# Two-layer hybrid encoder on one Trainium2 core: delta rule statistics and first matrices inside the short convolution's projection, later pieces in other slots

## The chip, the cores and the metric

The kernel runs on one core of a Trainium2 chip. The metric is the device time of one execution in microseconds (us). Engines are named as in the profile: PE (TensorE, matrix products; PEld its weight loads), DVE (VectorE), ACT (ScalarE), POOL (GpSimd) and SP (SyncE, which issues the loads of the weight stream).

## The reference, cut to what matters

The network has two layers, each a mixer, a cross attention over 256 memory rows and a squared-ReLU MLP, on 256 tokens of width 2048, all in float32. The change touches the even layer's mixer alone:

```python
def even_mixer(h, w_in, w_out, conv_qkv, a_log, dt_bias, out_gain, conv_sc):
    p = h @ w_in
    qkv = jax.nn.silu(centred_dwconv(p[..., :c1], conv_qkv))
    q = l2_normalize(q) * (DN_HEAD_DIM ** -0.5)
    k = l2_normalize(k)
    beta = jax.nn.sigmoid(ab[:, :, 0:2])
    g = -jnp.exp(a_log) * jax.nn.softplus(ab[:, :, 2:4] + dt_bias)
    o_fwd = gated_delta_rule(q, k, v, g[:, :, 0], beta[:, :, 0])
    o_bwd = flip(gated_delta_rule(flip(q), flip(k), flip(v), flip(g[:, :, 1]), flip(beta[:, :, 1])))
    ...
    y_sc = b_gate * centred_dwconv(c_gate * u_in, conv_sc)
    return jnp.concatenate([y_dn, y_sc], axis=-1) @ w_out
```

`gated_delta_rule` needs, for each chunk of tokens and each of 8 heads and 2 directions, the cumulative sums of g, the matrix `exp(diff)` of their differences, the products k k' and q k' scaled by it, and the inverse of the unit triangular matrix 1 + beta k k' exp(diff). With the inverse it runs over the chunks and carries a 128x128 state. The short convolution (`y_sc`) takes three other column blocks of the same projection and shares nothing with the delta rule but the output projection.

## The kernel before

**The weight stream.** All large products take their weights from one stream of units (128x1024 floats). SP loads them into a ring `raw`; for each unit ACT writes a rounded copy `split_hi` (`write_hi`, L330) when the unit four before it has been used, DVE writes the rest `split_lo` (`write_lo`, L337), and PE forms three reduced-precision products. PE counts used units in `s_used`. ACT and DVE run their other work between these copies, in the order in which the program lists it: `hi_upto(n)` and `lo_upto(n)` write the copies up to unit n, and what is listed behind them waits.

**The projection.** `pe_even` runs six chunks for q, k, v (`ev_qkv`), two for the gate, and six for the short convolution (`ev_sc`, `column_chunk`, L428 to L430). A chunk has 8 units of 24 matmuls of 128x256 each. Chunks use banks 0 and 1, or 2 and 3 of PSUM by turns; banks 4 to 7 (`aux`) are idle meanwhile. ACT takes chunks 0 and 3 of `ev_sc` (`cgate`), DVE multiplies chunks 1 and 4 into it (L1600) and convolves (L1535, L1539), and multiplies chunks 2 and 5 with the result (L1608).

**The head of the delta rule** stands behind the last chunk. PE turns k and v (L1284, 32 transposes), forms the cumulative sums (L1293) and the squared norms of q (L1299). ACT and DVE take the turned k and v (L1475, L1614), DVE squares k and sums it (L1619, L1620), and a chain of small operations on `st` ends in `s_stats`. Then come the first matrices of group 0: `pe_delta_pre` (L1370) broadcasts the cumulative sums and the betas by a product whose left side is one column of `decay_g` or `brk`, repeated 128 times, in float32 (pieces `cum` and `beta`), and forms k k' and k q' (pieces `kk` and `kq`). DVE makes the differences (`dve_delta_diff`, L1694), ACT their exponentials (`act_delta_pre`, L1516), DVE the products with beta (L1702), with q k' (L1704) and with k k' (`dve_delta_AT`, L1710). ACT copies the diagonal blocks (`act_delta_diag`), POOL masks them (L1097), DVE starts the inverse (`dve_inv_first`, L1173 and L1175).

**The four groups.** A group is two heads in both directions. `pe_inv` inverts its four matrices in six levels. In a level, for each direction, PE forms a product (L1108, 64x64 quadrants), ACT copies it (L1156), PE forms the second (L1135) and DVE subtracts it (L1193) and transposes (L1197); the last level is L1113, L1122, L1185. PE has four slots in a level (0 to 23 in a group), ACT and DVE two (0 to 11). Three tables say in which slots the other work goes: the tail of the group before (`pe_delta_tail`: five steps, L1388, L1394, L1400, L1406, L1417 to L1419), and the pieces of the next group.

```python
DN_PE = {'tail': (0, 2, 5, 7, 9), 'cum': (0, 12), 'beta': (6, 18), 'kk': (0,), 'kq': (10,)}
DN_ACT = {'tail': (0, 1, 3), 'pre': (4, 9), 'diag': (9, 11)}
DN_DVE = {'R': 1, 'out': 4, 'squares': 5, 'diff': (1, 7), 'masks': (5, 8), 'AT': (7, 9), 'first': (9, 11)}
```

The first number of a pair is direction 0's slot, the second direction 1's. POOL clears the inverse's two areas (L1202), masks, multiplies q (L1760) and makes the values of a group (L1748).

## Time and profile before

| what | value |
|---|---|
| time, median of 3 runs | 2865.39 us (2865.32 to 2878.22) |
| time of the profiled execution | 2865.1 us |
| its span | 2863.3 us |
| PE busy | 2766.4 us (97%), 18050 matmuls |
| PEld busy | 2430.6 us (85%) |
| DVE busy | 1555.8 us (54%) |
| ACT busy | 1303.0 us (46%) |
| POOL busy | 119.6 us (4%) |
| chain that ended last | PE 91%, DVE 5%, ACT 2%, issue 1% |

The share of the busy time of PE says little here, since its matmuls overlap and since the whole kernel is a string of stages. What an edit is worth stands in the chain of waits of its own stage: for the even mixer that is from 216.8 us, where the short convolution's projection starts, to 527.2 us, where the output projection does.

### The profile page before, as it was taken

How to read it: one execution, taken by the hardware profiler on the slowest of the kernel's cores; microseconds unless marked ns; L12 is line 12 of the kernel's file. 1: busy time of each engine (PE TensorE's matmuls, PEld its weight loads, DVE VectorE, ACT ScalarE, POOL GpSimd, SP SyncE). 2: the span in 40 equal slices, each digit the busy share in tenths (PEclk: the TensorE clock that was granted, in tenths of full speed). 3: DMA queues.
4: the chain of work that ended last, by engine and by line, in shares of the span. 5: the costliest groups of instructions: out<-in, count | busy, mean ns of one | idle time of the engine just before them, and what ended most of it. 6: DMA issues, size and time to landing. Idle time of an engine off the chain costs nothing.

```text
span 2863.3 us, 44423 instructions
## 1 busy us (share of the span) xinstructions
PE 2766.4 (97%) x18050; PEld 2430.6 (85%) x18050; DVE 1555.8 (54%) x2080; ACT 1303.0 (46%) x1726; POOL 119.6 (4%) x167
## 2 busy tenths in 40 slices
PE   8999989999999999999999998799999999999999
PEld 8999978778888888888899898688888888888887
DVE  5555455575555555555544556654654555555554
ACT  4543333464553544435444444333654445354453
POOL 0000033000000000000000000250000000000000
PEclk9999987899999999999999999897999999999999
DMA  7455400444455555555544554002534555555554
GB/s 277 164 189 189 165 2 2 156 173 143 170 191 195 188 196 179 202 193 180 195 141 173 194 191 159 1 2 75 183 144 173 190 180 200 197 187 193 185 187 146
DMA packets 67801, 461.71 MB, mean 161 GB/s; under 512 B 7023, under 2 KB 10223, under 8 KB 13084
## 3 DMA queue, kind: packets, MB, share of 16 engines
q1 hardware_dynamic: 63824, 449.46, 43.8%
q10 hardware_dynamic: 3500, 5.21, 0.5%
q0 software_dynamic: 288, 4.19, 0.4%
q8 instruction: 158, 2.59, 0.4%
q14 instruction: 31, 0.25, 0.0%
HBM read 456.72 MB, written 5.27 MB: 161 GB/s over the span
## 4 chain that ended last, share of the span: by engine, by line
PE 91%; DVE 5%; ACT 2%; issue 1%; DMA 0%; ACTq 0%; POOL 0%; DVEq 0%; POOLq 0%
PE bank L405 17%; PE bank L386 13%; PE bank L388 13%; PE bank L387 13%; PE bank L407 9%; PE bank L428 5%; PE bank L430 5%; PE bank L429 5%; PE bank L1108 1%; PE bank L1135 1%; PE bank L1370 1%; DVE split_lo L337 1%; PE bank L2227 1%; ACT split_hi L330 0%; DVE hT L578 0%
## 5 line engine op out<-in xcount | busy, mean ns | idle before, releaser
L337 DVE TENSOR_TENSOR split_lo<-raw,split_hi 128x1024 fp32r<-128x1024 f32 x840 | 1019.7, 1224 | 964.2 <-ACT split_hi L330 963.9
L330 ACT ACTIVATE split_hi<-raw 128x1024 fp32r<-128x1024 f32 x840 | 881.1, 1058 | 1168.6 <-PE bank L388 576.3
L405 PE MATMUL bank<-hT,split_hi 128*128 128x512 f32 x2048 | 716.1, 394 | 1.5 <-DVE hT L578 1.5
L407 PE MATMUL bank<-hT,split_lo 128*128 128x256 f32 x2048 | 573.7, 280 | 0.7 <-issue 0.7
L405 PEld LDWEIGHTS bank<-hT,split_hi 128*128 128x128 f32 x2048 | 383.8, 187 | 92.1 <-issue 2.3
L386 PE MATMUL bank<-split_hi,u_hi 128*128 128x512 f32 x1152 | 449.4, 390 | 0.0
L388 PE MATMUL bank<-split_hi,u_lo 128*128 128x512 f32 x1152 | 448.4, 389 | 0.0
L387 PE MATMUL bank<-split_lo,u_hi 128*128 128x512 f32 x1152 | 448.3, 389 | 0.0
L407 PEld LDWEIGHTS bank<-hT,split_lo 128*128 128x128 f32 x2048 | 386.6, 189 | 1.8 <-issue 1.7
L428 PE MATMUL bank<-hT,split_hi 128*128 128x256 f32 x1328 | 377.8, 284 | 3.1 <-DVE hT L578 1.8
L430 PE MATMUL bank<-hT,split_lo 128*128 128x256 f32 x1328 | 377.2, 284 | 0.0
L429 PE MATMUL bank<-hT,split_hi 128*128 128x256 f32 x1328 | 377.1, 284 | 0.0
L428 PEld LDWEIGHTS bank<-hT,split_hi 128*128 128x128 f32 x1328 | 256.4, 193 | 3.7 <-DVE hT L578 2.0
L429 PEld LDWEIGHTS bank<-hT,split_hi 128*128 128x128 f32 x1328 | 256.3, 193 | 0.2
L430 PEld LDWEIGHTS bank<-hT,split_lo 128*128 128x128 f32 x1328 | 256.3, 193 | 0.0
L388 PEld LDWEIGHTS bank<-split_hi,u_lo 128*128 128x128 f32 x1152 | 216.2, 188 | 45.1
L387 PEld LDWEIGHTS bank<-split_lo,u_hi 128*128 128x128 f32 x1152 | 216.3, 188 | 44.6
L386 PEld LDWEIGHTS bank<-split_hi,u_hi 128*128 128x128 f32 x1152 | 216.3, 188 | 44.5
L386 PE MATMUL bank<-split_hi,hT 128*128 128x512 f32 x448 | 175.9, 393 | 1.9 <-DVE split_lo L337 1.3
L387 PE MATMUL bank<-split_lo,hT 128*128 128x512 f32 x448 | 175.0, 391 | 0.0
L388 PE MATMUL bank<-split_hi,hT 128*128 128x512 f32 x448 | 174.8, 390 | 0.0
L386 PEld LDWEIGHTS bank<-split_hi,hT 128*128 128x128 f32 x448 | 84.5, 189 | 20.4 <-DVE split_lo L337 2.2
(446 smaller groups left out, 2336.3 us busy)
## 6 DMA issues: line engine op xcount, KB each, us to landing
raw<-in_stream SPq DMA_DIRECT2D x420, 1024.0 KB, 4.8
work<-in_mem POOLq DMA_DIRECT2D x2, 2048.0 KB, 8.4
bias_rows<-bias_line SPq DMA_DIRECT2D x1, 3072.0 KB, 14.2
hwork<-bias_rows ACTq DMA_DIRECT2D x2, 1536.0 KB, 9.8
x<-in_x SPq DMA_DIRECT2D x1, 2048.0 KB, 9.2
out<-x SPq DMA_DIRECT2D x4, 512.0 KB, 5.0
rwork<-in_wide ACTq DMA_DIRECT2D x1, 1280.0 KB, 13.9
const<-in_masks SPq DMA_DIRECT2D x1, 1121.5 KB, 13.5
```

What stands on the lines that cost most here:

```text
L330: nc.scalar.activation(split_hi[:, u % SPLIT], raw[:, b % RAW, (u % 2) * UNIT:(u % 2 + 1) * UNIT], ACT.Copy).then_inc(s_hi, 1)
L337: nc.vector.tensor_tensor(split_lo[:, u % SPLIT], raw[:, b % RAW, (u % 2) * UNIT:(u % 2 + 1) * UNIT], f32(split_hi[:, u % SPLIT]), SUB).th ...
L386: nc.tensor.matmul(out, lhsT=x_hi, rhs=w_hi[:, cols], start=k == 0, stop=False)
L387: nc.tensor.matmul(out, lhsT=x_hi, rhs=w_lo[:, cols], start=False, stop=False)
L388: m = nc.tensor.matmul(out, lhsT=x_lo, rhs=w_hi[:, cols], start=False, stop=k == k_tiles - 1)
L405: nc.tensor.matmul(out[:, :], lhsT=w_hi[:, cols], rhs=hT[:, k].rearrange("p two s -> p (two s)"), start=k == 0, stop=False)
L407: m = nc.tensor.matmul(out[:, S:2 * S], lhsT=w_lo[:, cols], rhs=hT_hi[:, k, :], start=False, stop=k == KD - 1)
L428: nc.tensor.matmul(out, lhsT=w_hi[:, cols], rhs=hT_hi[:, k, :], start=k == 0, stop=False)
L429: nc.tensor.matmul(out, lhsT=w_hi[:, cols], rhs=hT_lo[:, k, :], start=False, stop=False)
L430: m = nc.tensor.matmul(out, lhsT=w_lo[:, cols], rhs=hT_hi[:, k, :], start=False, stop=k == KD - 1)
L1108: i = nc.tensor.matmul(aux[d][rows, m * HALF:(m + 1) * HALF], lhsT=mask[rows, d, m, :], rhs=T[rows, d, m, :], start=True, stop=True)
L1135: i = nc.tensor.matmul(out, lhsT=lhsT, rhs=rhs, start=True, stop=True)
```

## The change

Five parts.

1. The transposes of v and of k, the cumulative sums, the squares of q and the statistics are done inside the six chunks of `ev_sc`. PE does a piece behind a given unit of a chunk (`pe_delta_head`); ACT and DVE have their share placed between copies of the stream (`hi_sc`, `lo_sc`). v is now taken by ACT (before: DVE). The banks are 4 to 7.
2. The broadcasts of the cumulative sums and the betas take another form, for all groups. Once for all heads and both directions, a float32 product writes the sums (and later the betas) as rows; ACT rounds them (`act_rows_hi`), DVE writes the rest to other partitions of the same tile `rowsT` (`dve_rows_lo`). A piece is then 2 reduced-precision products of 128x256, whose left side is a column of the constant `pick`, where it was 4 float32 products of 128x128.
3. Group 0's pieces are formed behind unit 3 of chunk 4 (`cum`, `beta`) and behind unit 0 of chunk 5 (`kk`, `kq`, in banks 0 and 1, once chunk 4 has been taken). Its differences, exponentials, masks and the start of its inverse go between the copies of chunks 4 and 5. POOL's first masks come ahead of its clearing, which waits for the end of the projection.
4. Buffers move, since the head's tiles may no longer lie over the stream's ring or over `hT`: they take the room of the memory's keys and values, which is free then (`mwork`).
5. In the slots of groups 1 to 3, direction 0's differences (DVE) go from 1 to 0, its beta (PE) from 6 to 2, the tail's third product (PE, L1400) from 5 to 3, and direction 0's diagonal (ACT) from 9 to 8.

```diff
-        DN_PE = {'tail': (0, 2, 5, 7, 9), 'cum': (0, 12), 'beta': (6, 18), 'kk': (0,), 'kq': (10,)}
-        DN_ACT = {'tail': (0, 1, 3), 'pre': (4, 9), 'diag': (9, 11)}
-        DN_DVE = {'R': 1, 'out': 4, 'squares': 5, 'diff': (1, 7), 'masks': (5, 8), 'AT': (7, 9), 'first': (9, 11)}
+        DN_PE = {'tail': (0, 2, 3, 7, 9), 'cum': (0, 12), 'beta': (2, 18), 'kk': (0,), 'kq': (10,)}
+        DN_ACT = {'tail': (0, 1, 3), 'pre': (4, 9), 'diag': (8, 11)}
+        DN_DVE = {'R': 1, 'out': 4, 'squares': 5, 'diff': (0, 7), 'masks': (5, 8), 'AT': (7, 9), 'first': (9, 11)}
...
+        def pe_delta_head(pe, c, u):
+            if (c, u) == (0, 1):
+                pe.wait_ge(s_silu, 6)
+                pe.wait_ge(s_abv, 2)
+                pe_delta_turn(pe, dn_vT)
+            elif (c, u) == (1, 2):
+                pe_delta_turn(pe, dn_kT, taken=True)
+            elif (c, u) == (2, 2):
...
+                m.then_inc(s_head_pe, 1)
+            elif (c, u) == (4, 0):
+                pe.wait_ge(s_stats, 1)
+                pe.wait_ge(s_kv_a, 8)
+                for t in range(NT):
+                    m = nc.tensor.matmul(aux[3][:, t * P:(t + 1) * P], lhsT=eightfold(brk_rows, t), rhs=ident, start=True, stop=True)
+                m.then_inc(s_head_pe, 1)
+            elif (c, u) == (4, 3):
+                pe.wait_ge(s_head_act, 1)
+                for d in range(2):
+                    for piece in ("cum", "beta"):
+                        pe_delta_pre(pe, 0, d, piece)
+            elif (c, u) == (5, 0):
+                wait_chunks_taken(pe, starts["ev_sc"][0] + 5)
+                for piece in ("kk", "kq"):
+                    pe_delta_pre(pe, 0, 0, piece)
...
+            if hp == 1 and piece == "kk":
+                wait_chunks_taken(pe, after("ev_sc"))
...
+                if piece in ("cum", "beta"):
+                    own = pick[:, 8 * d + h:8 * d + h + 1].broadcast_to([P, P])
+                    m = nc.tensor.matmul(out[:, i * S:(i + 1) * S], lhsT=own, rhs=rowsT[:, d if piece == "cum" else 2, :],
+                                         start=True, stop=True)
+                    continue
...
+            lo_sc(4, 5)
             for d in range(2):
                 dve_delta_diff(dve, 0, d)
-                dve_delta_masks(dve, 0, d)
+            lo_sc(4, 8)
+            for d in range(2):
+                dve_delta_DB(dve, 0, d)
+            take_gated(4)
+            for d in range(2):
+                lo_sc(5, 1 + d)
+                dve_delta_QKT(dve, 0, d)
+            for d in range(2):
+                lo_sc(5, 3 + d)
                 dve_delta_AT(dve, 0, d)
             for d in range(2):
                 dve_inv_first(dve, 0, dn_inv[0], d)
+            take_output(5)
...
         def pool_even(pool):
-            pool.wait_ge(s_stats, 1)
+            pool_delta_masks(pool, 0)
+            wait_chunks_taken(pool, after("ev_sc"))
             for Tf in dn_Tt:
                 m = pool_clear(Tf)
             m.then_inc(iv_clear, 1)
-            pool_delta_masks(pool, 0)
```

Three places show how the rows move. The first is PE behind the last matmul of the projection, before: all of the head, then group 0's first product (L1108). A float32 product counts once in these rows and is two instructions in the trace; a transpose counts once in both.

```order
L1284 MATMUL bank<-const,work 128x128 x32
L1293 MATMUL bank<-st,const 128x8 x8
L1299 MATMUL bank<-const,hwork 128x1 x16
L1370 MATMUL bank<-const,st 128x128 x8
L1370 MATMUL bank<-work 128x128 x8
L1370 MATMUL bank<-const,st 128x128 x8
L1108 MATMUL bank<-work 64x64 x8
L1370 MATMUL bank<-const,st 128x128 x4
L1370 MATMUL bank<-work 128x128 x4
L1108 MATMUL bank<-work 64x64 x8
```

The same place now (L436 to L438 are the projection's matmuls, L1116 the inverse's first product, L1423 the new broadcasts, L1428 k k'):

```order
L437 MATMUL bank<-hT,split_hi 128x256
L438 MATMUL bank<-hT,split_lo 128x256
L1116 MATMUL bank<-work 64x64 x8
L1423 MATMUL bank<-rowsT,pick 128x256 x2
L1428 MATMUL bank<-work 128x128 x4
L1116 MATMUL bank<-work 64x64 x8
L1143 MATMUL bank<-work 64x32 x8
L1423 MATMUL bank<-rowsT,pick 128x256 x2
L1143 MATMUL bank<-work 64x32 x8
```

Nothing of the head is left between the projection and the inverse; it stands between units of the projection, as this one, behind unit 2 of chunk 2 (sums, rows, squares of q):

```order
L438 MATMUL bank<-hT,split_lo 128x256
L1366 MATMUL bank<-st,const 128x8 x8
L1372 MATMUL bank<-const,work 128x128 x4
L1378 MATMUL bank<-const,mwork 128x1 x16
L436 MATMUL bank<-hT,split_hi 128x256
```

The second place is DVE in chunk 5, now (L345 copies of the stream, L1805 and L1811 group 0's products with q k' and k k', L1181 and L1183 the start of its inverse, L1688 the taking of chunk 5):

```order
L345 TENSOR_TENSOR split_lo<-raw,split_hi 128x1024
L1805 SCALAR_TENSOR_TENSOR mwork<-bank,st,mwork 128x128 x4
L345 TENSOR_TENSOR split_lo<-raw,split_hi 128x1024
L1811 SCALAR_TENSOR_TENSOR mwork<-bank,st,mwork 128x128 x4
L345 TENSOR_TENSOR split_lo<-raw,split_hi 128x1024
L1811 SCALAR_TENSOR_TENSOR mwork<-bank,st,mwork 128x128 x4
L1181 TENSOR_TENSOR work<-const,work 128x256
L1183 STREAM_TRANSPOSE work<-work 128x256
L1181 TENSOR_TENSOR work<-const,work 128x256
L1183 STREAM_TRANSPOSE work<-work 128x256
L1688 TENSOR_TENSOR work<-work,bank 128x512 x2
```

Both starts of the inverse stand ahead of the taking of chunk 5, where before they stood behind it and behind the whole head.

The third place is PE in the first two levels of group 1, before:

```order
L1388 MATMUL bank<-hwork,rwork 128x128 x4
L1370 MATMUL bank<-const,st 128x128 x4
L1370 MATMUL bank<-work 128x128 x4
L1108 MATMUL bank<-hwork,work 64x64 x8
L1135 MATMUL bank<-work,hwork 64x32 x8
L1394 MATMUL bank<-hwork 128x128 x4
L1135 MATMUL bank<-work,hwork 64x32 x8
L1108 MATMUL bank<-hwork,work 64x64 x16
L1400 MATMUL bank<-hwork,work 128x128 x4
L1135 MATMUL bank<-work,hwork 64x32 x8
L1370 MATMUL bank<-const,st 128x128 x4
L1135 MATMUL bank<-work,hwork 64x32 x8
```

and now (L1447, L1453, L1459 are the tail's first three steps):

```order
L1447 MATMUL bank<-hwork,rwork 128x128 x4
L1423 MATMUL bank<-rowsT,pick 128x256 x2
L1428 MATMUL bank<-work 128x128 x4
L1116 MATMUL bank<-hwork,work 64x64 x8
L1143 MATMUL bank<-work,hwork 64x32 x8
L1453 MATMUL bank<-hwork 128x128 x4
L1423 MATMUL bank<-rowsT,pick 128x256 x2
L1143 MATMUL bank<-work,hwork 64x32 x8
L1459 MATMUL bank<-hwork,work 128x128 x4
L1116 MATMUL bank<-hwork,work 64x64 x16
```

The third step of the tail comes ahead of the second level's first products, and each broadcast is 2 rows of 128x256 where it was 4 of 128x128.

## Rows read from the trace of the kernel before

**Rows 1.** Busy time in stretches; columns: us, PE, PEld, DVE, ACT, POOL, PEclk, DMA share, GB/s

```profile
216.80:355.00 138.20, 138.20 (x1153) 138.11 (x1151) 69.45 (x76) 50.62 (x51) 0.00 (x0) 1.00 0.51 180
355.00:383.10 28.10, 16.28 (x129) 15.93 (x129) 18.18 (x44) 11.66 (x18) 3.24 (x4) 0.81 0.00 1
383.10:407.40 24.30, 22.02 (x434) 20.26 (x434) 16.89 (x52) 8.60 (x22) 13.27 (x20) 0.92 0.01 3
407.40:443.70 36.30, 34.29 (x490) 31.82 (x490) 20.60 (x60) 11.43 (x29) 13.31 (x20) 0.78 0.01 2
```

**Rows 2.** The chain of waits between projection and inverse: start us, us, what

```profile
355.15 1.30 DVE work L1608 x2
...
356.69 3.70 PE bank L1284 x32
...
369.17 5.45 PE bank L1370 x32
```

**Rows 3.** Timeline of PE in the head: start us, us, engine, line, shapes, count

```profile
360.22 1.85 PE L1293 MATMUL bank<-st,const 128*128 128x8 f32 x16
361.92 3.71 PE L1299 MATMUL bank<-const,hwork 128*128 128x1 f32 x32
...
372.66 1.95 PE L1370 MATMUL bank<-work 128*128 128x128 f32 x16
```

**Rows 4.** The chain of waits in the projection: one matmul of 128x256

```profile
340.00 0.12 PE bank L428
```

**Rows 5.** Timeline of DVE about the end of chunk 4

```profile
334.35 1.28 DVE L1600 TENSOR_TENSOR work<-work,bank 128x512 f32<-128x512 f32 x2
335.66 1.14 DVE L1535 TENSOR_SCALAR work<-work,par 128x256 f32<-128x256 f32 x4
336.84 3.38 DVE L1539 SCALAR_TENSOR_TENSOR work<-work,par 128x256 f32<-128x256 f32 x8
```

**Rows 6.** Timeline of DVE in the head: product of group 0 with beta

```profile
379.32 0.69 DVE L1702 TENSOR_TENSOR rwork<-rwork,bank 128x512 f32<-128x512 f32 x1 [0.77 <-ACT rwork L1516]
```

**Rows 7.** Timeline of ACT: a change of function and what follows it

```profile
77.00 1.28 ACT L1436 ACT_TABLE_LOAD   x1
78.29 1.06 ACT L1436 ACTIVATE work<-work 128x1024 f32<-128x1024 f32 x1
```

**Rows 8.** Timeline of POOL, head and group 0

```profile
369.26 0.95 POOL L1202 MEMSET rwork<- 128x1024 f32 x1 [368.42 <-DVE st L1632]
...
384.53 1.58 POOL L1760 TENSOR_TENSOR hwork<-work,hwork 128x256 f32<-128x256 f32 x2
386.07 2.77 POOL L1097 TENSOR_TENSOR work<-iv_diag,const 128x256 f32<-128x256 f32 x4
```

**Rows 9.** The chain of waits in groups 0 to 3

```profile
388.92 1.07 PE bank L1108 x32
...
410.51 3.28 PE bank L1370 x16
...
419.25 1.09 PE bank L1370 x8
...
436.02 2.02 PE bank L1370 x8
```

**Rows 10.** Busy time in stretches of one granted clock; columns as in rows 1

```profile
386.80:406.80 20.00, 18.32 (x404) 16.66 (x402) 15.01 (x49) 7.63 (x20) 9.63 (x15) 1.00 0.01 2
...
413.70:434.00 20.30, 18.90 (x343) 17.31 (x344) 11.77 (x34) 5.02 (x12) 6.66 (x11) 1.00 0.01 2
434.00:447.70 13.70, 13.10 (x144) 12.31 (x139) 8.82 (x27) 6.25 (x16) 4.53 (x7) 0.50 0.01 2
447.70:468.40 20.70, 19.30 (x328) 17.71 (x329) 10.95 (x31) 4.67 (x11) 8.78 (x14) 0.99 0.01 3
468.40:488.70 20.30, 19.69 (x244) 18.33 (x244) 11.12 (x34) 7.72 (x19) 9.75 (x14) 0.50 0.00 1
488.70:505.80 17.10, 14.05 (x300) 12.80 (x297) 10.91 (x24) 7.09 (x13) 4.01 (x7) 1.00 0.04 7
```

More of the change, by code:

```diff
@@ L214, in R, with M @@
             return view(rwork, at, *shape)
+        def M(at, *shape):
+            return view(mwork, at, *shape)
         def four(ap):
@@ L1591, in dve_even, with lo_sc, take_gated @@
             dve.wait_ge(s_silu, 6)
-            for half in range(2):
-                c = 3 * half + 1
+            def lo_sc(c, used):
+                lo_upto(dve, min(chunk_done("ev_sc", c - 1) + used + AHEAD, starts["ev_out"][1]))
+            def take_gated(c):
                 banks, taken = chunk_banks("ev_sc", c)
-                lo_upto(dve, chunk_done("ev_sc", c - 1) + AHEAD)
-                lo_upto(dve, chunk_done("ev_sc", c) + AHEAD)
                 wait_chunks_taken(dve, starts["ev_sc"][0] + c)
```

218 lines of the change are left out of this document (129 added, 89 removed).

## The prediction, made before the changed kernel was run

> **What bounds the kernel now.** I read the busy time in stretches first, to see which part of the even mixer leaves PE without work. The projection of the short convolution has none to give: PE is busy for all of its 138.20 us at a granted clock of 1.00, while DVE is busy for 69.45 us, ACT for 50.62 and POOL not at all [rows 1]. The 28.1 us behind it are the opposite: PE 16.28, DVE 18.18, each waiting for the other, and no DMA [rows 1]. The chain of waits through this stretch is the second view: it goes from DVE's taking of the last chunk over PE's transposes (3.70 us) to the float32 broadcasts and products (5.45 us), with DVE and ACT between [rows 2]. Nothing in it needs the projection's result, but it stands behind it. Third, the chain through the groups: from the second level on it runs mostly over PE, and the broadcasts stand in it with 1.09 to 3.28 us each [rows 9]. So PE sets the end in the projection and mostly in the groups, and the head is a string of waits that could lie beside the projection.
>
> **The head goes away: 28.1 us off.** A sixth of the projection is 23.03 us, a unit 2.88 us. ACT and DVE need about half of that for the copies. If group 0's inverse is started when chunk 5 ends, PE goes from the last unit straight to its first product. Counted from the end of chunk 5's unit 4, DVE has one copy, one product with k k', ACT two diagonals, POOL the masks and DVE two starts to do; none is longer than 3 us, and 4 units (11.5 us) cover them. If that cover were gone the start would come late by what is missing, up to some 6 us.
>
> **What PE does instead, inside the projection: 13.4 us on.** PE has no idle time there, so each of its instructions counts in full. The 32 transposes take 3.70 [rows 2]. The sums (x16) took 1.85 and the squares (x32) 3.71; by their starts 1.70 and 3.7 [rows 3]. Products of 128x128 in float32 cost 1.95 us for 16 instructions at full clock, 0.12 each [rows 3]: the rows of the sums are 8 instructions, 0.96; the rows of the betas 4, 0.48; `kk` and `kq` 16, 1.95. The new broadcasts are 8 products of 128x256 in the projection's own form, at 0.12 each [rows 4]: 0.96. Together 13.45 us. No row shows this form with a single repeated column on its left side; at the least it costs nothing, at the most what the float32 form costs, 3.9 us for the 32 instructions it replaces. I take the projection's row, since type and shape are the same.
>
> **A new wait at the third piece: 2.2 us on.** `kk` and `kq` of group 0 write banks 0 and 1, so PE waits behind unit 0 of chunk 5 until DVE has taken chunk 4. Chunk 4 ends at 216.8 + 5 x 23.03 = 331.95. The taking ran from 334.35 to 335.63 [rows 5]; now two products with beta of 0.69 us stand ahead of it [rows 6], so it ends at 337.0. PE is there at 331.95 + 2.88 = 334.8. That is 2.2 us of idle PE; the whole rest of the projection is queued behind it. Bounds: 0, if ACT's and DVE's copies keep their times and the products with beta get ahead of the last copy; and 5, if ACT's exponentials push its copies back by their own length.
> ACT changes function three more times in the projection's time. A change took 1.28 us, and the next activation began 1.29 us after its start [rows 7]. The Trainium skill, ScalarE: Activation LUTs, section What ACT_TABLE_LOAD costs, puts a switch at about 2.66 us, with a drain behind the load. The trace does not agree for this kernel: the row has no drain in it. By the page the copies ahead of the taking would come about 1 us later and the sum would be 1 us less of a gain.
>
> **Do the copies of the stream stay ahead?** A copy may start once the unit four before it is used, and PE needs it three units, 8.6 us, later. The longest new stretch without a copy on DVE is two products with beta, the taking (1.28) and the convolution (1.14 and 3.38) [rows 5, 6], 7.2 us, begun 2.4 us behind chunk 4's end; it ends at 9.6, the next copy is done by 10.9, and PE needs it at 11.5 without the wait above and at 15.7 with the wait and the 1.95 of `kk` and `kq`. I cost it at nothing; the cover is 0.6 to 4.8 us.
>
> **Group 0: 2.0 us off.** Its first product starts at full clock, but POOL's clearing must now wait for the end of the projection. From there: taking of chunk 5 1.3 and a hand-over of 0.15 [rows 2], two clearings of 0.95, two products of q 1.58, the first mask of level 2 at 2.77 / 4 = 0.7 [rows 8]: 5.6 us. Before, level 2 began at 388.92, 5.8 us behind the first product at 383.1 [rows 1, 9], so the start gives nothing; POOL is late next. Two broadcasts leave the path of levels 2 to 4, 8 instructions and 1.09 each before, now nothing (it falls into POOL's wait) and 0.24: 1.9 us. The last third of the group is DVE's, and DVE's work is the same.
>
> **Groups 1 and 2: 3.2 us off each.** In slot 0 broadcast and `kk` took 3.28 us, half of it for each at mostly half clock [rows 9]; `kk` stays, the broadcast becomes 0.5: 1.0 off. Direction 0's beta was 1.09, now 0.4: 0.7 off. Direction 1's beta was 2.02, with DVE waiting for it, now 0.5: 1.5 off [rows 9]. Direction 1's sums lie beside DVE's work and count as nothing. Group 2 repeats the pattern. Of the moved slots, the differences and the third product feed waits on DVE and ACT that are not on the chain while PE is; I cost them at nothing, between a gain of 1 us per group and the same as a loss. Group 3 has no pieces of a next group: nothing.
>
> **The clock: 3.3 us on.** The granted clock in the groups changes between its two levels, 2.4 GHz (1.00) and 1.2 GHz (0.50). In group 1 it was 0.50 for 13.7 us and in group 2 to 3, where fewer and smaller products stand, for 20.3 us, with PE busy for 13.10 and 19.69 of them [rows 10]. It fell each time behind a stretch at 1.00 in which PE had been idle for 1.4 us in all (18.90 of 20.30, 19.30 of 20.70) [rows 10], and rose late. The change takes 128x128 work out of just these stretches. I charge the difference of these two stretches once, 6.6 us at half clock, 3.3 us. The bounds are a gain of 6.6 (the first of them vanishes, half of 13.10) and the last rival below.
>
> **Sum:** -28.1 + 13.45 + 2.2 - 2.0 - 2 x 3.2 + 3.3 = -17.5 us. The profiled execution took 2865.1 us, so 2847.6; the median of the runs, 2865.39, is the same within 0.3 us. A measurement of this kernel can tell about 0.5%, 14.3 us, from no change.
>
> **The rivals.**
> B, the groups give nothing: DVE's chain closes up behind what PE gives back. For it: DVE is busy for 16.89 of 24.30 us in group 0 and 20.60 of 36.30 in group 1 [rows 1], and the end of each group is its own. Against it: the chain's own rows are PE's. 2865.1 - 28.1 + 13.45 + 2.2 = 2852.7.
> C, the clock helps: denser groups keep the full clock through the first of the slow stretches, and nothing is charged. 2847.6 - 3.3 - 6.6 = 2837.7. For it, only that the idle time in the stretches that ended in a fall was short, 1.4 us, and may close.
> D, the stream starves: with a cover of as little as 0.6 us, some of the five stretches of head work on DVE and ACT overrun it by about 1 us each, and the clock falls once more. 2847.6 + 5 + 3.3 = 2855.9. Against it, DVE is half idle there [rows 1].
> E, slower: the clock stays at half level through the groups. Its place is the four stretches of 20.0, 20.3, 20.7 and 17.1 us at 1.00, in which PE was busy for 70.6 us [rows 10]. Less the 8.4 us taken out, 62 us of PE's work would take twice as long: 2847.6 + 62 = 2910. It outweighs the gain once some 18 of these 62 us are lost. For it: the 0.50 from group 2's end on lasted 20.3 us, with PE busy for 19.69 of them [rows 10]. Against it: the clock rose in group 3 too, at 488.7, where no piece of a next group stands [rows 10]. The Trainium skill, TensorE: Matmul & The Clock Gate, section What's actually happening, says that the throttled state is the default and that activity releases it. By that rule, less work on PE speaks for E; the trace agrees so far as the longest stretch at 0.50 is the one with the fewest products of 128x128.
>
> **How the numbers follow.** Forecast A 0.62, B 0.14, C 0.12, D 0.07, E 0.05. The likeliest is A, 2847.6, with its own range from 2841 (no wait at the third piece, no charge for the clock) to 2852 (the wait at 5 us, the moved slots a small loss). The range for 8 in 10 reaches beyond it, to 2836 for C and to 2856 for D: left out are E, half of D and half of C, 0.15. Faster by over 0.5% (below 2851) are A but for 0.06, C and a little of B: 0.70. Within 0.5% are the rest of A, B and D: 0.26. Slower is E but for 0.01: 0.04.
>
> **What would show it.** In the profile of the changed kernel the stretch between the last 128x256 matmul of the projection and the first 64x64 product should be below 0.5 us; the projection should last 138.2 + 13.45 + 2.2 = 153.9 us, with one idle time of PE of about 2 us at the k k' product that DVE's taking of chunk 4 ends; PE should wait in level 2 of group 0 for POOL's mask, by about 1 us; the new broadcasts should read 0.12 us each at clock 1.00; and groups 1 and 2 should last about 33 us each instead of 36.3. Waits of the projection's matmuls for `split_lo` would show D, a clock of 0.50 where rows 10 have 1.00 would show E. The forecast is wrong if the time is outside 2836 to 2856.

## The result, and the profile of the changed kernel

The changed kernel took 2855.08 us (median of 9 runs, 2852.31 to 2861.01), the kernel before in the same comparison 2866.44 us (9 runs). The ratio is 0.995, with a 95% interval of 0.9936 to 0.9964. A second comparison on another chip gave 2855.38 us against 2868.89 us, 0.9958 (0.9944 to 0.9972). So the change gains 11 to 14 us, 0.4 to 0.5%. The forecast was 17.5 us. The time lies inside the range of 2836 to 2856 us, at its slow end.

The page of the changed kernel: span, busy time, clock in 40 slices, and the chain by engine.

```profile
span 2851.4 us, 44270 instructions
PE 2762.2 (97%) x17966; PEld 2421.5 (85%) x17966; DVE 1555.6 (55%) x2080; ACT 1305.0 (46%) x1733; POOL 119.6 (4%) x167
PEclk9999996899999999999999999897999999999999
PE 92%; DVE 4%; ACT 2%; issue 1%; DMA 0%; ACTq 0%; POOL 0%; DVEq 0%; POOLq 0%
```

The profiled execution took 2853.17 us, 11.9 us less than that of before. PE's busy time fell by 4.2 us only, since most of what went was waiting and the head's work moved rather than went. The seventh clock slice reads 6: the groups' clock has its own part in what follows.

The busy time in stretches, the changed kernel: the projection with the head in it, then groups 0 to 3. They answer to [rows 1]; columns as there.

```profile
215.80:372.70 156.90, 154.73 (x1271) 154.36 (x1272) 86.33 (x119) 64.19 (x75) 3.07 (x4) 0.98 0.45 159
372.70:395.96 23.26, 19.00 (x408) 16.67 (x409) 16.65 (x52) 8.74 (x23) 13.53 (x20) 0.96 0.01 3
395.96:429.10 33.14, 29.63 (x464) 27.03 (x465) 20.49 (x60) 11.28 (x28) 13.32 (x20) 0.81 0.01 2
429.10:463.01 33.91, 31.24 (x464) 28.82 (x464) 20.67 (x60) 11.27 (x28) 13.32 (x20) 0.75 0.01 2
463.01:513.78 50.77, 44.29 (x497) 40.84 (x498) 20.10 (x44) 17.61 (x33) 12.34 (x18) 0.60 0.11 43
```

And the two last of them in the kernel before, which [rows 1] does not reach:

```profile
443.70:479.46 35.76, 33.76 (x489) 31.39 (x489) 20.60 (x60) 11.14 (x28) 13.30 (x20) 0.79 0.01 2
479.46:527.20 47.74, 40.06 (x497) 36.47 (x498) 19.85 (x44) 17.61 (x33) 12.35 (x18) 0.69 0.12 45
```

The ledger, from [rows 1] and these rows:

| stretch | before | after | difference | forecast |
|---|---|---|---|---|
| projection and head | 166.3 | 156.9 | -9.4 | -12.45 |
| group 0 | 24.3 | 23.3 | -1.0 | -2.0 |
| group 1 | 36.3 | 33.1 | -3.2 | -3.2 |
| group 2 | 35.8 | 33.9 | -1.9 | -3.2 |
| group 3 and last tail | 47.7 | 50.8 | +3.0 | 0 |
| the groups' clock | | | (in the rows above) | +3.3 |
| all else | | | +0.6 | 0 |
| span | 2863.3 | 2851.4 | -11.9 | -17.5 |

Two places lost what was not foreseen: the projection, which now runs at a granted clock of 0.98 instead of 1.00, and group 3, whose clock went from 0.69 to 0.60. The chain of waits of the changed kernel shows the first, and the foreseen waits beside it (start us, us, what):

```profile
274.21 1.69 PE bank L1366 x16
275.89 0.99 PE bank L1372 x8
276.88 5.31 PE bank L1378 x32
...
332.99 0.91 PE bank L1423 x8
...
349.13 1.30 DVE work L1678 x2
350.47 2.05 PE bank L1428 x16
...
372.71 1.29 DVE work L1688 x2
374.12 0.95 POOL rwork L1210
375.07 0.89 POOL work L1210
375.95 1.38 POOL hwork L1861 x2
377.33 0.69 POOL work L1105
378.16 0.68 PE bank L1116 x16
...
399.08 0.43 PE bank L1423 x2
399.51 1.70 PE bank L1428 x8
...
456.64 0.74 PE bank L1423 x2
```

L1366 are the sums, L1372 the rows and L1378 the squares of q. The squares took 5.31 us, where they took 3.71 [rows 3]. The broadcasts (L1423) are 8 products in 0.91 us. Behind the squares the matmuls of the projection take 0.21 us each up to 285.2 us, and 0.12 again from there. L1428 (`kk`, `kq`) stands behind DVE's taking of chunk 4 (L1678), and the first level-2 product (378.16) behind POOL's clearings, products and mask, as the forecast has it.

What PE waited for between 215 and 515 us, changed kernel: us in total, times, longest.

```profile
PE bank L1116 <- DVE hwork L1201: 3.2, 3, 2.0
...
PE bank L1428 <- DVE work L1678: 2.2, 1, 2.2
...
PE bank L1116 <- POOL work L1105: 0.8, 1, 0.8
```

No matmul of the projection waited for `split_lo` or `split_hi`: the stream did not starve. Here is the clock in one stretch in which PE does nothing but the later squares, in one behind it with the projection's own matmuls, and in one of the same length a little later:

```profile
278.60:282.19 3.59, 3.59 (x18) 3.59 (x18) 0.00 (x0) 0.00 (x0) 0.00 (x0) 0.50 0.54 224
282.20:285.50 3.30, 3.30 (x18) 3.30 (x19) 0.00 (x0) 0.00 (x0) 0.00 (x0) 0.57 0.00 0
286.00:289.30 3.30, 3.30 (x29) 3.30 (x29) 1.70 (x2) 1.06 (x1) 0.00 (x0) 1.00 0.00 0
```

PE reads as busy for all three. The clock is at its lower level in the first and in most of the second. The squares cost 1.6 us more than their row. Behind them 18 matmuls are counted in 3.3 us where 29 are at full clock, 11 x 0.12 = 1.3 us more. Together 2.9 us, which is the projection's shortfall of 3.0 within 0.1.

### The profile page after: what moved, and what is told of

The parts are those of the page before. It is cut to its first block, busy times and chain, and to the rows that moved or that the text cites. A ratio compares the mean times of both kernels' runs of the same rounds, so it can differ in the third digit from the quotient of the medians.

```text
span 2851.4 us, 44270 instructions
## 1 busy us (share of the span) xinstructions
PE 2762.2 (97%) x17966; PEld 2421.5 (85%) x17966; DVE 1555.6 (55%) x2080; ACT 1305.0 (46%) x1733; POOL 119.6 (4%) x167
## 4 chain that ended last, share of the span: by engine, by line
PE 92%; DVE 4%; ACT 2%; issue 1%; DMA 0%; ACTq 0%; POOL 0%; DVEq 0%; POOLq 0%
PE bank L413 17%; PE bank L394 13%; PE bank L395 13%; PE bank L396 13%; PE bank L415 8%; PE bank L436 5%; PE bank L438 5%; PE bank L437 5%; PE bank L1116 1%; PE bank L1143 1%; ACT split_hi L338 1%; PE bank L2328 1%; DVE split_lo L345 1%; DVE hT L586 0%; PE bank L1982 0%
## 5 line engine op out<-in xcount | busy, mean ns | idle before, releaser
L345 DVE TENSOR_TENSOR split_lo<-raw,split_hi 128x1024 fp32r<-128x1024 f32 x840 | 1020.1, 1224 | 967.8 <-ACT split_hi L338 967.1
L436 PE MATMUL bank<-hT,split_hi 128*128 128x256 f32 x1328 | 377.5, 284 | 3.1 <-DVE hT L586 1.8
L438 PE MATMUL bank<-hT,split_lo 128*128 128x256 f32 x1328 | 376.3, 283 | 0.0
L436 PEld LDWEIGHTS bank<-hT,split_hi 128*128 128x128 f32 x1328 | 255.5, 192 | 3.7 <-DVE hT L586 2.0
L438 PEld LDWEIGHTS bank<-hT,split_lo 128*128 128x128 f32 x1328 | 255.4, 192 | 0.0
```

What stands on the lines that cost most here:

```text
L345: nc.vector.tensor_tensor(split_lo[:, u % SPLIT], raw[:, b % RAW, (u % 2) * UNIT:(u % 2 + 1) * UNIT], f32(split_hi[:, u % SPLIT]), SUB).th ...
L436: nc.tensor.matmul(out, lhsT=w_hi[:, cols], rhs=hT_hi[:, k, :], start=k == 0, stop=False)
L438: m = nc.tensor.matmul(out, lhsT=w_lo[:, cols], rhs=hT_hi[:, k, :], start=False, stop=k == KD - 1)
```

## The experiments

All times are medians with the ratio to the kernel before on the same chip, which itself read 2866.4 to 2869.4 us. The stretches come from each run's own profiled execution. "Half clock" is worked out from 1 us stretches as the sum of 2 x (1 - granted clock); "later" is what follows the output projection's start, which no kernel here changes. Where a text below gives the stretches of single groups, they run from the first product of one tail (L1447 in the changed kernel) to that of the next, about 1 us behind the group's own start, and the last one to the output projection.

| kernel | time | ratio (95%) | head | groups | half clock in them | later | half clock, second mixer |
|---|---|---|---|---|---|---|---|
| before | | | 166.4 | 143.8 | 64.5 | 2336.4 | 71.6 |
| after | 2855.08 | 0.995 (0.9936, 0.9964) | 156.8 | 140.8 | 71.4 | 2337.9 | 78.5 |
| after_again | 2855.38 | 0.9958 (0.9944, 0.9972) | 156.7 | 141.9 | 68.3 | 2338.2 | 78.5 |
| squares_split | 2851.18 | 0.9927 (0.9907, 0.9946) | 155.2 | 140.6 | 71.4 | 2340.7 | 85.4 |
| third_later | 2853.89 | 0.9941 (0.992, 0.9962) | 154.3 | 140.1 | 71.6 | 2342.2 | 88.7 |
| both_head | 2850.95 | 0.995 (0.9932, 0.9968) | 151.2 | 140.1 | 71.5 | 2340.4 | 85.3 |
| old_slots | 2860.68 | 0.9971 (0.9952, 0.999) | 158.2 | 138.4 | 61.4 | 2345.0 | 99.0 |
| head_alone | 2862.36 | 0.9973 (0.9961, 0.9986) | 155.1 | 141.8 | 58.0 | 2342.8 | 78.5 |
| both_tail5 | 2852.04 | 0.9949 (0.9933, 0.9965) | 151.2 | 137.4 | 58.0 | 2346.5 | 99.0 |
| both_tail5_pool | 2853.43 | 0.9944 (0.9925, 0.9963) | 151.2 | 138.7 | 61.4 | 2343.7 | 99.0 |
| both_tail5_busy | 2847.52 | 0.9939 (0.9919, 0.9959) | 151.1 | 135.1 | 37.5 | 2340.1 | 71.7 |
| busy_wide | 2834.40 | 0.9883 (0.9862, 0.9904) | 151.2 | 128.2 | 13.6 | 2336.7 | 78.5 |
| before_busy | 2859.04 | 0.9967 (0.9949, 0.9985) | 166.4 | 132.7 | 20.3 | 2343.6 | 88.7 |
| after_busy | 2841.82 | 0.9908 (0.9886, 0.993) | 158.2 | 125.4 | 6.8 | 2336.0 | 75.1 |

The column "later" has to be read first. Nothing in it was changed, yet it varies by 10 us, and mostly with the half clock of the second layer's mixer. Between two kernels, the stretches of the head and the groups tell more than the medians do. In the table the groups end with the first matmul of the output projection, 0.3 us ahead of where the ledger's rows end. A ratio rests on 4 to 11 runs of a kernel; only the intervals of busy_wide and after_busy lie clear of that of the changed kernel.

**1. squares_split: the squares in four pieces, behind units 3 to 6.**

```diff
-                for t in range(NT):
-                    for h in range(DN_H):
+            elif c == 2 and u in (3, 4, 5, 6):
+                t = (u - 3) // 2
+                for h in range(4 * ((u - 3) % 2), 4 * ((u - 3) % 2) + 4):
```

> The 16 one-column products (squares of q) stand behind unit 2 of chunk 2 in one run; here four each stand behind units 3, 4, 5 and 6. In the trace of the changed kernel the granted clock is at 0.50 from 278.6 to 285.9 us, beginning 1.7 us into these products. Theory A (a run of products of one column lets the clock fall): the clock stays at 1.00 through the projection, the first 64x64 product of group 0 comes 3.4 us earlier after the projection's start (156.8 us to about 153.4), and the time falls by about 3 us. Rival B (the fall has another cause, the interruption of the stream as such or the moment): there is still a stretch at 0.50 of about 7 us in the projection, and the time is the same.

The head took 155.2 us, 1.6 less than the changed kernel and 1.8 more than expected. The clock stayed at 1.00 behind the squares, but fell for 3.4 us behind the wait for chunk 4 instead:

```profile
277.00:290.00 13.00, 13.00 (x114) 13.00 (x113) 9.31 (x7) 3.17 (x3) 0.00 (x0) 1.00 0.43 163
351.40:354.90 3.50, 3.50 (x19) 3.50 (x18) 3.43 (x10) 0.00 (x0) 0.00 (x0) 0.51 0.22 91
```

So the squares in one run are what lowers the clock at 278 us, and a second weak place lies behind it. The kept traces bear this out: the clock fell in or right behind the squares in all eight in which they stand in one run (the kernel before and before_busy among them), and in none of the six in which they stand in four pieces. At the wait of 2.2 us for chunk 4 it fell in three of six (squares_split, old_slots, after_busy). The squares follow directly on the sums, 16 instructions of 8 columns, and on the rows; whether the squares alone would lower the clock was not tried.

**2. third_later: `kk` and `kq` of group 0 one unit later.**

```diff
-            elif (c, u) == (5, 0):
+            elif (c, u) == (5, 1):
```

> Group 0's products k k' and k q' go from behind unit 0 to behind unit 1 of chunk 5. The wait of 2.2 us for DVE's taking of chunk 4 was 5.2 us behind the end of chunk 4, and unit 1 ends 5.8 us behind it. Theory A (the wait is only a matter of place): PE's wait goes, the projection with the head is 2.2 us shorter (156.8 to 154.6), nothing is later at the start of group 0, time 2 us less. Rival B (the wait moves on): DVE's products with q k' are pushed back behind the later PE products, the start of the inverse comes too late, and PE waits at the first 64x64 product instead; time the same or more.

The head took 154.3 us, 2.5 less, and the wait of 2.2 us is gone, as theory A has it; DVE's later work is still in time. The median fell by 1.2 us only. What remained before `kk` was a wait of 0.4 us for the taking of chunk 5, in group 1.

**3. both_head: both edits.**

> Both head edits together: the squares of q in four parts behind units 3 to 6 of chunk 2, and group 0's k k' and k q' behind unit 1 of chunk 5. Each alone left one stretch at half clock in the projection: with the squares in parts it came behind the 2.2 us wait (351 to 355), with the later third piece behind the squares (278 to 285). Theory A (both falls are set off by what stands just before them: a run of one-column products, a pause of PE of 2 us): no half clock between 216 and the inverse, projection with head 138.2 + 13.4 = 151.6 us (changed kernel 156.8), and about 5 us less in time than the changed kernel. Rival B (falls come at some rate whatever stands there): one stretch remains, 153.5 us or more.

The head took 151.2 us. This is its busy time in both_head:

```profile
215.90:367.10 151.20, 151.20 (x1271) 151.07 (x1271) 86.30 (x119) 64.42 (x75) 2.88 (x4) 1.00 0.46 164
```

And this one of the four pieces of the squares in the chain of waits of both_head:

```profile
279.77 0.79 PE bank L1380 x8
```

PE is busy throughout at a clock of 1.00, and 8 squares cost 0.79 us. The forecast's 138.2 + 13.45 without wait and clock is 151.65 us; the sum of the PE work is right within 0.5 us. Up to the output projection both_head is 6.3 us shorter than the changed kernel, and the later part was 2.5 us longer in the profiled run. The median is 4 us lower than on the changed kernel's chip, but the ratio to the kernel before is 0.995 in both: the gain is shown by the stretches and not by the times.

**4. old_slots: the four table moves undone, everything else of the change kept.**

```diff
-        DN_PE = {'tail': (0, 2, 3, 7, 9), 'cum': (0, 12), 'beta': (2, 18), 'kk': (0,), 'kq': (10,)}
+        DN_PE = {'tail': (0, 2, 5, 7, 9), 'cum': (0, 12), 'beta': (6, 18), 'kk': (0,), 'kq': (10,)}
```

(and `diag` from 8 to 9, `diff` from 0 to 1)

> The changed kernel with the tables of slots as before (third product of the tail in slot 5, beta in 6, direction 0's differences on DVE in 1, its diagonal on ACT in 9). I forecast nothing for the moved slots. Theory A: groups 0 to 2 the same within 0.5 us each, group 3 with its tail (50.8 us in the changed kernel, 47.7 before) the same, so that its 3.1 us of loss are the clock's. Rival B: the third product in slot 3 runs at the half clock in group 3 (2.0 us instead of 1.1) and causes the loss: group 3 comes back to 48 us here, and the time is 2 to 3 us less.

Groups 0 to 2 lasted 24.5, 33.1 and 34.1 us, those of the changed kernel 24.4, 33.1 and 33.9: the moves do nothing there. The last stretch lasted 46.7 us against 49.4: with the moves it is 2.7 us longer. Its head lasted 158.2 us, since the clock fell behind the squares and once more behind the wait for chunk 4. Even so old_slots is the quicker kernel by the stretches, by 1 us up to the output projection. By the medians it is the slower one (2860.68, the intervals overlap), and its granted clock over all its runs was 0.9696 on average against 0.9707. Whether the moves bring something through the later clock is not settled.

**5. head_alone: also the broadcasts of groups 1 to 3 in their old form.**

```diff
-                if piece in ("cum", "beta"):
+                if piece in ("cum", "beta") and hp == 0:
...
+                    if piece == "cum":
+                        lhsT = decay_g[:, t, 8 * d + h:8 * d + h + 1].broadcast_to([P, P])
+                        rhs = const_of("causal", 2 * d + 1)
```

> Groups 1 to 3 are as in the kernel before (float32 broadcasts of 4 products, the old slots); only the head and group 0's own matrices are inside the projection. Theory A (the sum by parts holds): groups 0 to 3 last what they lasted before, 24.3, 36.3, 35.8 and 47.7 us, so the kernel keeps the head's gain of 9.6 us alone, ratio to the kernel before 0.9966, and the clock in groups 1 to 3 has the stretches of before. Rival B (the groups' new form and slots give the net gain and the head little, or entering group 0 at full clock changes the pattern after it): the stages of the groups differ by more than 1 us each from before.

The stretches from group 0 on were 25.9, 35.6, 36.3 and 44.0 us, against 24.5, 33.1, 34.1 and 46.7 in old_slots. The new form takes 6.1 us off the groups in which it stands and gives 2.7 back in the last, which has none: net 3.4. The kernel before has 25.3, 36.3, 35.8 and 46.4 us by the same cuts, so the last stretch of head_alone is 2.4 us shorter than there with the same instructions in it, at 22.8 us of half clock against 28.6. Theory A fails there: what stands earlier shifts the clock of the groups. The head lasted 155.1 us, the clock behind the squares having fallen for only 3.4 us in this run instead of 6.8; that depth is not the program's alone.

**6. both_tail5: both_head, with the tail's third product back in slot 5.**

```diff
-        DN_PE = {'tail': (0, 2, 3, 7, 9), 'cum': (0, 12), 'beta': (2, 18), 'kk': (0,), 'kq': (10,)}
+        DN_PE = {'tail': (0, 2, 5, 7, 9), 'cum': (0, 12), 'beta': (2, 18), 'kk': (0,), 'kq': (10,)}
```

> As both_head, and of the four moved slots only the tail's third product back in slot 5. With all four undone the stretch from group 2's tail to the output projection was 46.7 us, against 49.4 in the changed kernel. Theory A (the third product in slot 3 is what costs group 3, where no piece of a next group stands): 46.7 us or less again, groups 0 to 2 as in the changed kernel, time 2.7 us below both_head. Rival B (it is one of the others, or the phase of the clock): 49 us again.

Group 3 with the last tail in both_head:

```profile
457.90:507.10 49.20, 42.87 (x482) 39.54 (x481) 20.04 (x44) 16.86 (x31) 12.21 (x18) 0.60 0.12 44
```

and in both_tail5:

```profile
457.70:504.40 46.70, 38.86 (x483) 35.38 (x481) 19.85 (x44) 16.87 (x31) 12.23 (x18) 0.69 0.12 46
```

This one move sets the clock of the last stretch: 0.69, as before the change, against 0.60. The stretch is 2.5 us shorter. The other traces agree: in the five with slot 3 and no unused products it has 39.0 to 39.5 us of half clock and lasts 49.2 to 50.4 us, in the five with slot 5 it has 22.8 to 29.1 us and lasts 44.0 to 46.8. The median did not follow (2852.04 against 2850.95), and the later part was 6.1 us longer in the profiled run.

**7. both_tail5_pool: also POOL's second clearing and its products with q behind the masks of levels 2 and 3 of group 0.**

```diff
-            for Tf in dn_Tt:
-                m = pool_clear(Tf)
+            pool_clear(dn_Tt[0])
...
+                    if hp == 0 and level == 3:
+                        pool_clear(dn_Tt[1]).then_inc(iv_clear, 1)
+                        for d in range(2):
+                            pool_delta_pre(pool, 0, d)
```

> As both_tail5, and POOL clears only the first area ahead of the masks of levels 2 and 3 of group 0; the second clearing and the two products of q come behind them. In the changed kernel PE waited 0.8 us for POOL's first mask of level 2, and the chain there went over POOL for 4 us. Theory A (POOL is what is late at the start of group 0): group 0 is 0.8 to 2 us shorter (23.3 to about 22). Rival B (DVE's differences in its slot 0 are as late as POOL): the wait goes over to DVE, group 0 the same.

The wait for POOL (0.8 us) is gone, and in its place stands one for DVE, kernel both_tail5_pool:

```profile
PE bank L1116 <- DVE work L1201: 0.6, 1, 0.6
```

The stretch from group 0's start to the first tail was 24.4 us instead of 24.8. POOL was late, but DVE was almost as late: 0.4 us at the most. Over the four groups nothing was won: 138.7 us against 137.4, with 3.4 us more of half clock in them.

**8. both_tail5_busy: both_tail5 with 16 unused float32 products of 128x256, four each in slot 19 of group 0 and slot 15 of groups 1 to 3.** Nothing is left out; `pe_keep_busy` issues products into a bank that nobody reads, and both kernels call it in other stages already.

```diff
+                    n = {(0, 19): 4, (1, 15): 4, (2, 15): 4, (3, 15): 4}.get((hp, slot), 0)
+                    pe_keep_busy(bank[1], n)
```

> As both_tail5, with four unused float32 products of 128x256 (1.7 us at full clock) in PE's pause of each group: slot 19 of group 0, slot 15 of groups 1 to 3. They write a free bank; nothing reads it. Theory A (PE's pause of 1.5 to 2 us lets the clock fall and the fall costs the groups several us each): the stretches at half clock behind the pauses (7, 14 and 21 us in groups 1, 2 and 3) go or shrink, groups 1 to 3 are 3 to 6 us shorter each, time 8 us or more below both_tail5. Rival B (the thin mix of 64x64 products lets it fall whether PE pauses or not): the same stretches at half clock, and the time is up by what the products delay, 0 to 3 us.

Half clock in the groups fell from 58.0 to 37.5 us and their time from 137.4 to 135.1, though PE has more to do. The expected 3 to 6 us for each of groups 1 to 3 did not come: the four stretches are 25.6, 32.1, 33.8 and 43.6 us against 24.8, 32.6, 33.3 and 46.7, so the last alone gains. The median fell by 4.5 us where 8 were expected; the two intervals overlap.

**9. busy_wide: both_tail5_pool with 21 such products at six slots and one behind each of the last tail's first four steps.**

```diff
+                    n = {(0, 19): 3, (1, 15): 4, (1, 19): 3, (2, 15): 4, (2, 19): 3, (3, 15): 4}.get((hp, slot), 0)
...
+                if step < 4:
+                    pe_keep_busy(bank[3], 1)
```

> As both_tail5_pool, with unused float32 products in both pauses of PE in every group (slot 19: three, in groups 0 to 2; slot 15: four, in groups 1 to 3) and one behind each of the last four waits of the last tail. With fillers in one pause of each group the half clock from the projection to the output projection went from 58.0 to 37.5 us and the stretch from 288.6 to 286.2 us. Theory A (pauses of 1.6 us let the clock fall in each group): less than 20 us at half clock, stretch 280 us or less, granted clock of the whole run 0.980 or more, and by the slope of 19 us of time for 0.01 of clock that the runs of every kernel here show, a time of about 2843. Rival B (the remaining falls come from the thin mix of 64x64 products): still 35 us or more at half clock, and the stretch is longer by what the fillers delay.

**10. after_again: the changed kernel on the same chip, as a yardstick.**

> The changed kernel itself once more, so that it stands beside busy_wide on one chip. Theory A: stages as in the first trace within 0.5 us each up to the output projection (projection with head 156.8, groups 33.1 and 33.9, last stretch 49.4), the half clock in the projection behind the squares again; the time differs by what the second layer's mixer, untouched by the change, spends at half clock. Rival B: the stages themselves move by several us from run to run.

busy_wide took 2834.40 us, 0.9883 (0.9862 to 0.9904), and beats both kernels: 21 us less than after_again (2855.38), 34 less than before. It is 9 us faster than expected; half clock in the groups is 13.6 us and the stretch from the projection to the output projection 279.4 us, as theory A has it. In after_again the head and groups 0 to 2 lasted what they had lasted in the first trace within 0.2 us, but the last stretch 50.4 us instead of 49.4, and the half clock in groups 1 to 3 lies in other places. So a stretch of one trace can move by 1 us with nothing changed. All this left open whether the products need the change.

**11 and 12. before_busy and after_busy: the 25 products of experiment 9 (the texts of the expectations count the 21 in the slots as 18) in the kernel before, and in the changed kernel, with no other edit.**

> The kernel before with the wide set of unused products in the groups (18 at six slots, 4 in the last tail), nothing of the change in it. Theory 1, the products act only through the clock of the groups and the gain has nothing to do with the change: the 75 us at half clock between 200 and 520 us fall to below 35 us, of which most stand in group 1 to 3; the stretches of the groups get shorter by some 14 us together and the time is 2866 - 14 = 2852 us. Theory 2, the products help only where the new broadcasts have taken the float32 ones away (four float32 products of 128x128 keep the clock by themselves, so that there is less to win): the half clock stays above 55 us and the time is 2860 us or more.

> The changed kernel with the same wide set of unused products in the groups and no other edit. Theory 1: the head keeps its two losses (squares at half clock, wait for chunk 4, together 5.6 us), the third product its slot 3, the groups and the last tail run as with the full set: 2834.4 + 5.6 + up to 2.5 = 2840 to 2843 us. Theory 2, slot 3 and the POOL order matter more than the clock: above 2848 us.

Groups 0 to 3, kernel before_busy:

```profile
383.20:408.00 24.80, 23.88 (x454) 21.78 (x454) 16.89 (x52) 8.97 (x23) 13.29 (x20) 0.94 0.01 3
408.00:439.90 31.90, 31.09 (x509) 27.90 (x503) 20.42 (x60) 11.30 (x28) 13.34 (x20) 1.00 0.01 2
439.90:471.70 31.80, 30.99 (x504) 27.88 (x502) 20.41 (x60) 11.24 (x28) 13.33 (x20) 1.00 0.01 3
471.70:515.90 44.20, 38.40 (x500) 33.92 (x497) 19.42 (x44) 16.67 (x33) 12.36 (x18) 0.81 0.12 49
```

and kernel after_busy:

```profile
375.00:398.80 23.80, 20.83 (x431) 18.17 (x430) 16.65 (x52) 9.15 (x24) 13.54 (x20) 1.00 0.01 3
398.80:429.50 30.70, 28.64 (x483) 25.36 (x479) 20.39 (x60) 11.33 (x28) 13.34 (x20) 1.00 0.01 2
429.50:460.10 30.60, 28.54 (x480) 25.34 (x478) 20.39 (x60) 11.23 (x28) 13.33 (x20) 1.00 0.01 3
460.10:500.40 40.30, 34.51 (x500) 30.32 (x496) 19.49 (x44) 16.44 (x32) 12.35 (x18) 0.92 0.15 54
```

By the half clock theory 1 holds: it fell to 20.3 us in the kernel before, and the products act through the clock, with or without the change. They take 11.1 us off the groups of before and 15.4 off those of after. The median of before_busy, 2859.04 us, is 7 us above what was expected, and close to theory 2's 2860; 2.9 us of that are missing in the groups (11.1 instead of 14), and the later part was 7.2 us longer in the profiled run (2343.6 against 2336.4 us). after_busy, 2841.82 us, is where theory 1 put it.

The rows also show what the change does to a group when the clock stays up: groups 1 and 2 last 30.7 and 30.6 us instead of 31.9 and 31.8, 1.2 us less each. With the products in both kernels the change is worth 15.5 us up to the output projection, as against 12.6 without them: part of its gain had gone into the clock. The medians give 17.2 us (2859.04 to 2841.82) as against 11 to 14, but on 8 and 4 runs and with later parts that differ by 7.6 us. Slot 3 for the third product is no loss here. Group 3 with the last tail lasts 40.3 us with slot 3, and 41.8 in busy_wide with slot 5, where it has 3.4 us more of half clock. A kernel with both_head's two edits and after_busy's groups was not tried.

## Why the prediction was right in part

**The head: right.** The stretch between the projection and the inverse is gone: its last matmul starts at 372.4 us, the first 64x64 product at 372.6 (forecast below 0.5 us apart). The 28.1 us went.

**The work on PE inside the projection: right in amount, wrong in one term.** Sums 1.69 us (forecast 1.70), rows 0.99 (0.96), broadcasts 0.91 (0.96); both_head's 151.2 us for the whole. The failed term is "the squares (x32) 3.71". The row was taken over as a duration, as if the place did not matter. The squares took 5.31 us and the matmuls behind them 1.3 us more than at full clock, since the clock fell during the squares; together 2.9 us. Here lies the miss in the head. The trace of before held the warning. These are a stretch inside the squares there, which ended at 365.63 us, one right behind them, and the longer one up to `kk` and `kq` at 372.66 us:

```profile
363.60:365.60 2.00, 2.00 (x19) 1.95 (x18) 1.97 (x2) 1.02 (x1) 0.00 (x0) 1.00 0.00 0
365.70:367.70 2.00, 0.00 (x0) 0.00 (x0) 1.97 (x3) 0.00 (x0) 0.00 (x0) 0.51 0.00 0
365.00:373.00 8.00, 4.46 (x26) 4.38 (x26) 4.80 (x13) 2.00 (x3) 1.84 (x2) 0.57 0.00 0
```

The clock had fallen there too, within 0.1 us of their end and ahead of the 3.5 us in which PE then stood idle, so the pause is not what set it off. What that cost lay inside the 28.1 us that were to go, and I read only the duration.

**The wait at the third piece: right.** 2.2 us forecast, 2.2 measured, from the same releaser; third_later took it away.

**The copies stay ahead: right.** No wait for the stream. The change of ACT's function at 293.34 us again took 1.28 us with the next activation 1.30 us behind its start, as in [rows 7]. This is its row and the next, the timeline of ACT in the changed kernel:

```profile
293.34 1.28 ACT L1546 ACT_TABLE_LOAD   x1
294.64 0.26 ACT L1546 ACTIVATE st<-st 128x64 f32<-128x64 f32 x1
```

**Group 0: half of it.** Level 2 began 5.5 us behind the projection's end (forecast 5.6, before 5.8), behind POOL's mask, with a wait of 0.8 us. So 0.3 of the group's 1.0 us came from its start, and the 1.9 us for the two broadcasts came out as 0.7. Of the 1.2 missing POOL has 0.4 at the most (both_tail5_pool); where the other 0.8 went was not separated.

**Groups 1 and 2: the step "3.2 us off each" mixed two things.** It came out in group 1 (3.2) and not in group 2 (1.9), and the match in group 1 is luck in part: its granted clock rose from 0.78 to 0.81, while that of group 2 fell from 0.79 to 0.75. Two of its three terms were taken from rows at half clock (3.28 and 2.02 us [rows 9]). In a group at full clock the same change takes 2.45 us of busy time off PE (31.09 to 28.64) and only 1.2 us off the group. Rival B, DVE's chain closing up, is right to that extent: in group 1 of the changed kernel PE is busy for 29.63 of 33.14 us, where it was 34.29 of 36.30 [rows 1], so 1.5 us of what PE gave up became waiting. The longest waits in the groups are those for DVE's L1201, 2.0 us at once.

**Group 3: "nothing" was wrong, +3.0 us.** It has no pieces of a next group, but it has the tail of group 2, whose third product moved from slot 5 to 3. That move was costed at nothing as a matter of waits; both_tail5 shows that it costs 2.5 us, at 10 us more of half clock, and after_busy that no such cost is left where the clock stays up. Why slot 3 brings more half clock than slot 5 was not shown.

**The clock: the size nearly right, by luck in part.** I charged 6.6 us more at half clock; the groups had 6.9 more (64.5 to 71.4). But the charge was put on group 2 to 3 for the loss of 128x128 work. By the experiments the new broadcasts bring the groups little or no more half clock in all (58.0 us in head_alone, 61.4 in old_slots, 64.5 before); the moved slots bring 10 (61.4 to 71.4), and the third product alone accounts for them (58.0 in both_tail5, 71.5 in both_head). The reading behind the charge does not hold either. The rows of [rows 10] are two of five falls in the groups before. A third is as long as the longer of them, and stands in the last tail:

```profile
505.70:526.10 20.40, 15.77 (x97) 14.13 (x94) 6.21 (x15) 7.57 (x14) 0.00 (x0) 0.50 0.25 100
```

It came behind a stretch at 1.00 with 3.05 us of idle PE [rows 10], not 1.4, and it has 49 instructions of 128x128, where the stretch of 20.3 us has 24 and that of 13.7 us 21. So the long stretches at 0.50 are not those with the fewest products of 128x128. The Trainium skill, TensorE: Matmul & The Clock Gate, section What's actually happening, has the throttled state as the default which activity releases. The runs agree: 25 unused products took the half clock of the groups from 71.4 to 6.8 us.

**The rivals.** C and E did not come. D gives nearly the measured time, 2855.9 us, by the wrong mechanism: no wait for a copy is in the trace. B, at 2852.7 us, is nearer to it than the forecast as well, and was right in part. The forecast's own range ended at 2852 us and its lower end, by its own terms, is 2842 and not 2841; the measured 2855.08 us is outside it. It is inside the range for 8 in 10 only because that was stretched to 2856 for D, which did not happen. That hit is luck. The stretches fell by 12.4 us against 17.5 forecast; of the 5.1 us between them 3.0 are in the projection (the squares), 1.0 in group 0, 1.3 in group 2 and 3.0 in group 3, less the 3.3 that had been charged for the clock. Faster by over 0.5% had 0.70; the two comparisons give 0.5 and 0.4%, so the result lies on that bound, rather on the other side of it.

## What to carry to other kernels

Work that is moved under a PE-bound stretch costs its instructions, and may cost the clock as well: before moving a run of products with one or few columns, ask what the clock does behind it, and spread the run between full matmuls. A row at half clock is no price for the work at full clock, so read each term's granted clock with its duration, and price the clock of a stage as a term of its own. Where a stage drops to half clock in short pauses, a handful of unused products placed in those pauses can be worth more than the work that a change saves; here 25 of them took 13 us off the changed kernel and 8 off the one before, while 16 in fewer places took 2 us off the groups.

## What the runs showed of the hardware

A busy PE is not enough for the full clock. In the 16 float32 products of 128x1 (32 instructions, right behind 16 of 128x8) PE is busy without a gap, and the granted clock went from 1.00 to 0.50; the same products in four pieces, with 24 matmuls of 128x256 between them, left it at 1.00. Transposes of 128x128 did not lower it, neither 16 in a row inside the projection, twice, nor these 32 in the head of the kernel before:

```profile
356.69:360.20 3.51, 3.51 (x32) 3.51 (x33) 0.00 (x0) 3.19 (x6) 0.00 (x0) 1.00 0.02 5
```

A stage that nobody touched takes another time. The second layer's mixer has the same program in all kernels. Over 350 us of it, busy time and granted clock were in the kernel before

```profile
1690.00:2040.00 350.00, 312.92 (x3117) 280.12 (x3115) 207.24 (x424) 141.06 (x269) 63.10 (x79) 0.90 0.24 84
```

and in old_slots

```profile
1690.00:2040.00 350.00, 314.08 (x3031) 277.81 (x3030) 200.23 (x411) 137.71 (x267) 63.05 (x79) 0.86 0.22 79
```

A clock of 0.90 against 0.86, with 3117 matmuls against 3031 in the same time. In the table, 99 us of half clock there go with 2344 to 2347 us for the later part (three kernels), 71.6 to 78.5 us with 2336 to 2338 in five traces and with 2340 and 2343 in two. Over 62 runs of the kernel before, time and mean granted clock go together (correlation -0.79, 20 us for each 0.01). So an edit of 2 or 3 us early in the program can be hidden by this, or seem to be several times its size. What decides it in a given run stays open.
